# Two-layer hybrid networks on one core: the gate and up products as a 512-column and a 256-column matmul

## What is computed

```python
def swiglu_2(x, w_gate, w_up, w_down):
    return (jax.nn.silu(x @ w_gate) * (x @ w_up)) @ w_down

for i in range(DEPTH):                                   # DEPTH = 2
    g = norm_gains[i]
    f = swiglu_2(rmsnorm_2(h, g[0]), ffn_gate[i, 0], ffn_up[i, 0], ffn_down[i, 0])
    h = h + MACARON * rmsnorm_2(f, g[1])
    ...
    f = swiglu_2(rmsnorm_2(h, g[4]), ffn_gate[i, 1], ffn_up[i, 1], ffn_down[i, 1])
    h = h + MACARON * rmsnorm_2(f, g[5])
```

## Time and profile before

| | |
|---|---|
| median of 3 runs | 1739.27 us (1738.97 to 1739.59) |
| the profiled execution's own time | 1738.88 us |
| span of its trace | 1737.2 us |
| granted TensorE clock, mean | 0.993 |
| PE busy | 1688.1 us (97%), 11882 matmuls |
| DVE busy | 1177.2 us (68%) |
| ACT busy | 897.5 us (52%) |
| DMA | 353.80 MB, mean 204 GB/s |

### The profile page before, as it was taken

How to read it: one execution, slowest core, us unless ns; L and a number is a source line. 1 busy time by engine, 2 the same in 40 slices (tenths; PEclk the granted TensorE clock), 3 DMA queues, 4 the chain that set the end, 5 groups by cost and what they waited for, 6 DMA issues and landing times.

```text
span 1737.2 us, 30015 instructions
## 1 busy us (share of the span) xinstructions
PE 1688.1 (97%) x11882; PEld 1574.2 (91%) x11882; DVE 1177.2 (68%) x1485; ACT 897.5 (52%) x1240; POOL 110.2 (6%) x161
## 2 busy tenths in 40 slices
PE   6999999999999999999999999999999999999997
PEld 4987999998899998999898899999999999899997
DVE  7999789867764458655776755577655575765556
ACT  4567443366544345434577534356434468644446
POOL 3010211100200000000011000000000003000000
PEclk9999999999999999999999999999999999999999
DMA  9894899947555554554441554544555452455551
GB/s 380 319 336 162 287 357 384 377 161 294 193 195 189 175 192 158 194 190 175 170 156 72 175 200 173 190 166 175 176 190 190 169 183 74 141 205 177 192 187 68
DMA packets 61924, 353.80 MB, mean 204 GB/s; under 512 B 6522, under 2 KB 9738, under 8 KB 27792
## 3 DMA queue, kind: packets, MB, share of 16 engines
q1 hardware_dynamic: 40064, 281.24, 45.1%
q0 software_dynamic: 18384, 66.66, 10.4%
q10 hardware_dynamic: 3392, 4.72, 0.9%
HBM read 349.45 MB, written 3.15 MB: 203 GB/s over the span
## 4 chain that ended last, share of the span: by engine, by line
PE 83%; DVE 9%; DMA 3%; issue 2%; ACT 2%; POOL 1%; DVEq 0%; SPq 0%; POOLq 0%; ACTq 0%
PE bank L501 25%; PE bank L502 25%; PE bank L503 25%; DVE w_lo L1595 2%; PE bank L533 2%; PE bank L535 2%; PE bank L534 2%; PE bank L688 1%; DMA work<-bias_rows 1%; DVE shared L1617 1%; DMA raw<-in_stream 1%; DVE work L1979 1%; POOL work L488 1%; PE bank L701 1%; DVE x L2193 0%
## 5 line engine op out<-in xcount | busy, mean ns | idle before, releaser
L501 PE MATMUL bank<-a_hi,w_hi 128*128 128x256 f32 x2648 | 755.0, 285 | 12.3 <-DVE a_lo L1766 4.4
L503 PE MATMUL bank<-a_hi,w_lo 128*128 128x256 f32 x2648 | 752.0, 284 | 0.0
L502 PE MATMUL bank<-a_lo,w_hi 128*128 128x256 f32 x2648 | 751.9, 284 | 0.0
L501 PEld LDWEIGHTS bank<-a_hi,w_hi 128*128 128x128 f32 x2648 | 510.9, 193 | 18.1 <-issue 10.3
L502 PEld LDWEIGHTS bank<-a_lo,w_hi 128*128 128x128 f32 x2648 | 511.0, 193 | 2.5 <-issue 0.2
L503 PEld LDWEIGHTS bank<-a_hi,w_lo 128*128 128x128 f32 x2648 | 510.7, 193 | 0.0
L1865 DVE TENSOR_TENSOR w_lo<-raw,w_hi 128x2048 fp32r<-128x2048 f32 x144 | 330.0, 2292 | 241.8 <-ACT w_hi L1184 241.8
L1184 ACT CAST w_hi<-raw 128x2048 fp32r<-128x2048 f32 x144 | 274.1, 1903 | 270.6 <-PE bank L503 270.6
L1595 DVE TENSOR_TENSOR w_lo<-raw,w_hi 128x2048 fp32r<-128x2048 f32 x122 | 279.2, 2292 | 80.9 <-ACT w_hi L1043 80.6
L1043 ACT CAST w_hi<-raw 128x2048 fp32r<-128x2048 f32 x121 | 229.7, 1907 | 56.2 <-PE bank L503 47.5
L501 PE MATMUL bank<-w_hi,hid_hi 128*128 128x512 f32 x548 | 214.7, 392 | 0.0
(11 more groups left out here) (259 smaller groups left out, 1872.4 us busy)
## 6 DMA issues: line engine op xcount, KB each, us to landing
raw<-in_stream SPq DMA_DIRECT2D x266, 1024.0 KB, 4.8
shared<-in_mods POOLq DMA_DIRECT2D x104, 512.0 KB, 6.9
grow<-in_rows POOLq DMA_DIRECT2D x12, 512.0 KB, 4.0
work<-in_mods POOLq DMA_DIRECT2D x8, 512.0 KB, 8.9
bias_rows<-work ACTq DMA_DIRECT2D x1, 2048.0 KB, 20.6
x<-in_x_t SPq DMA_DIRECT2D x1, 1024.0 KB, 5.9
x<-in_x_d ACTq DMA_DIRECT2D x1, 1024.0 KB, 6.2
work<-bias_rows ACTq DMA_DIRECT2D x1, 1024.0 KB, 18.4
```

What stands on the lines that cost most here:

```text
L501: pe.matmul(out, w_h, v_h, start=start, stop=False, skip_group_check=True)
L502: pe.matmul(out, w_h, v_l, start=False, stop=False, skip_group_check=True)
L503: return pe.matmul(out, w_l, v_h, start=False, stop=stop, skip_group_check=True)
```

## The change

Three things, all in the FFNs i = 2 to 5.

1. `a_hi` and `a_lo` become the two halves of one tile `a_both`, so that a chunk's high and low activations lie side by side, 512 columns. A new `wide_slab` takes the place of `feature_slab` for gate and up slabs: per chunk and m one matmul of 512 columns (high weights by high and low activations) and one of 256 columns (low weights by high activations) onto its first half. The two m now have a bank each, so a gate slab fills banks 0 and 1, an up slab 2 and 3, without a second pair. `two_sums` views a pair as (m, token, half).
2. VectorE first adds the two halves (`tensor_reduce`, 1024 sums to 512 numbers, into `gate_s` or `hid`) and counts `gate_summed` or `up_summed`; it then scales those in place. TensorE waits for these counts before the next gate or up slab.
3. VectorE's order: at an FFN's start the gate's addition stands ahead of two `w_lo` slabs and `pre_root` ahead of these; at its end `hidden_lo` stands ahead of the last `w_lo`.

```diff
-        bank = [ctx.enter_context(nc.psum_tensor(f"bank{i}", [P, 512], F32)) for i in range(8)]
+        bank_pair = [ctx.enter_context(nc.psum_tensor(f"banks{i}", [P, 1024], F32)) for i in range(4)]
+        bank = [bank_pair[i // 2][:, 512 * (i % 2):512 * (i % 2) + 512] for i in range(8)]
+
+        def two_sums(b):
+            return bank_pair[b][:, :].rearrange("p (m k s) -> p m s k", m=2, k=2)
...
-        a_hi = sb("a_hi", [P, LCH, S], F32R)
-        a_lo = sb("a_lo", [P, LCH, S], F32R)
+        a_both = sb("a_both", [P, LCH, 2, S], F32R)
+        a_hi, a_lo = a_both[:, :, 0, :], a_both[:, :, 1, :]
...
+            def wide_slab(slot, pair_of_banks, chunk_ready=None):
+
+                for c in range(CH):
+                    if chunk_ready is not None:
+
+                        pe.wait_ge(nl_ready, chunk_ready + c + 1)
+                    for m in range(2):
+                        w_h, w_l = weights(slot, c * 256 + m * P, P)
+                        out = bank[2 * pair_of_banks + m]
+                        pe.matmul(out[:, :], w_h, a_both[:, c].rearrange("p k s -> p (k s)"), start=(c == 0), stop=False, skip_group_check=True)
+                        mm = pe.matmul(out[:, 0:S], w_l, a_hi[:, c, :], start=False, stop=(c == CH - 1), skip_group_check=True)
+                return mm
...
+                        if i > 1:
+
+                            pe.wait_ge((gate_summed, up_summed)[k], (1 if j is None else j) + (f0 - 2 * FJ))
+                            wide_slab(slot + k, k).then_inc(slab_done, 1)
+                            continue
...
-                    feature_slab(b, bank[0], before(APPLY_CHUNKS, ap)).then_inc(slab_done, 1)
+                    wide_slab(b, 0, before(APPLY_CHUNKS, ap)).then_inc(slab_done, 1)
                     pe.wait_ge(lo_ready, b + 2)
-                    feature_slab(b + 1, bank[2]).then_inc(slab_done, 1)
+                    wide_slab(b + 1, 1).then_inc(slab_done, 1)
...
+                    dve.tensor_reduce(pair(gate_s[:, par, :]), two_sums(0), mybir.AxisListType.X, ALU.add).then_inc(gate_summed, 1)
...
+                    dve.wait_ge(gate_summed, j + (f0 - 2 * FJ + 1))
+                    dve.tensor_tensor(pair(gate_s[:, par, :]), pair(gate_s[:, par, :]), over_pre(), ALU.mult).then_inc(gate_scaled, 1)
...
-                        dve.tensor_tensor(pair(hid[:, par, :]), pair(bank[2 + par][:, :]), over_pre(), ALU.mult).then_inc(up_scaled, 1)
+                        dve.tensor_reduce(pair(hid[:, par, :]), two_sums(1), mybir.AxisListType.X, ALU.add).then_inc(up_summed, 1)
+                        dve.wait_ge(up_summed, j + (f0 - 2 * FJ + 1))
+                        dve.tensor_tensor(pair(hid[:, par, :]), pair(hid[:, par, :]), over_pre(), ALU.mult).then_inc(up_scaled, 1)
...
+                gate_sum(0, 0, b + 1, True)
                 split_to(b + 4)
                 if i == 0:
                     mod_half()
-                gate(0, 0, b + 1, True)
+                gate_scale(0, 0, True)
...
                 hidden(j, j % 2, b + 3 * j + 1)
-                split_to(b + 3 * j + 4)
+                if i < 2:
+                    split_to(b + 3 * j + 4)
                 hidden_lo(j, j % 2)
+                if i >= 2:
+                    split_to(b + 3 * j + 4)
...
                 turned_low(apply2(l, LA_PRE1), gain2(l, 0))
-                split_to(base2(l) + 3)
+                split_to(base2(l) + 2)
                 pre_root(4 * l)
-                split_to(base2(l) + 4)
                 ffn(2 + 2 * l, base2(l))
```

More of the change, by code:

```diff
@@ L352, in build @@
         gate_scaled, up_scaled = sem("gate_scaled"), sem("up_scaled")
+        gate_summed, up_summed = sem("gate_summed"), sem("up_summed")
         table_ready = sem("rope_over_rms_ready")
@@ L1831, in ffn, with gate_sum @@
                 v = 4 * ((i - 2) // 2) + (0 if i % 2 == 0 else 2)
-                def gate(j, par, done, first=False):
+                def gate_sum(j, par, done, first=False):
                     if i < 2:
@@ L1839, in gate, with gate_scale @@
                         dve.wait_ge(hid_done, j + (f0 - 1))
+                    dve.tensor_reduce(pair(gate_s[:, par, :]), two_sums(0), mybir.AxisListType.X, ALU.add).then_inc(gate_summed, 1)
+                def gate_scale(j, par, first=False):
+                    if i < 2:
+                        return
                     if first:
                         dve.wait_ge(row_ready, rows_made(v))
-                    dve.tensor_tensor(pair(gate_s[:, par, :]), pair(bank[par][:, :]), over_pre(), ALU.mult).then_inc(gate_scaled, 1)
+                    dve.wait_ge(gate_summed, j + (f0 - 2 * FJ + 1))
+                    dve.tensor_tensor(pair(gate_s[:, par, :]), pair(gate_s[:, par, :]), over_pre(), ALU.mult).then_inc(gate_scaled, 1)
+                def gate(j, par, done, first=False):
+                    gate_sum(j, par, done, first)
+                    gate_scale(j, par, first)
                 def hidden(j, par, up, first=False):
@@ L2358, in _ @@
                 turned_low(apply2(l, LA_PRE2), gain2(l, 4))
-                split_to(bf + 3)
+                split_to(bf + 2)
                 pre_root(4 * l + 2)
-                split_to(bf + 4)
                 ffn(3 + 2 * l, bf)
```

## The result

| | kernel before | changed kernel |
|---|---|---|
| time, median of 4 runs each | 1739.43 us (1738.97 to 1740.80) | 1729.30 us (1728.39 to 1731.07) |
| ratio | | 0.9937, 95% interval 0.9916 to 0.9959 |
| profiled execution | 1738.88 us, span 1737.2 | 1728.39 us, span 1726.7 |

The change makes the kernel faster: by 10.1 us (0.6%) between the medians, by 10.5 us in the profiled executions. The forecast was 22.5: right sign, inside the range, less than half the size.

A forecast was written before the change was run, and what follows sets the result against it. TensorE's matmul pace was taken to bound the second network's FFNs: 1738.88 - 23 (matmuls) + 0.5 (start of FFN i = 2) = 1716.4 us profiled, median 1716.8, range 1707 to 1730.

The forecast's parts named there:

- What bounds the kernel: In the second network's FFNs, the time one matmul takes until the next can start on TensorE sets the time.
- The matmuls: In gate and up slabs, two matmuls replace three of 119.9 ns each; 1408 pairs save 23 us, the middle of two readings.
- by neighbours of unlike width: Pair cost in wide slabs read from single steps between unlike widths: 340 ns, 19.7 saved, 27.7 us in all.
- by the steady runs: Pair cost in wide slabs read from runs of one width: 346.6 ns, 13.1 saved, 18.4 us in all.
- the end at 351.6 ns: Outer pair cost in wide slabs if every 512 costs what a run's first six do: 8.1 ns or 11.4 us saved.
- VectorE's additions: Additions of 1.28 us each on DVE hide beside TensorE in the FFN loop, with 3.8 and 4.2 us to spare.
- The end of an FFN: Behind the last up slab, `hidden_lo` ends at 4.5 us, wanted at 5.5, with the moved `w_lo` needed; cost 0.
- the rival of the seams: If an addition takes 2.56 us, FFN ends lose 0.4 us each and starts up to 2: 1719 to 1727; 7%.
- The start of an FFN: The gate's addition ahead of two `w_lo`, with rope angles in FFN i = 2, costs 0.5 us, once.
- The time by columns: Rival for wide slabs: time goes by columns, only a ns or two per matmul falls away; 1736 to 1739.3; 5%.
- VectorE the bound: Rival: strided additions make DVE the loop's bound; about 3.7 us each eats the gain, 4 gives about 1774 us; 3%.

The follow-up runs named there:

- e1: Changed kernel with three matmuls of 256 columns per product again in place of the wide and narrow pair; 1743.27 us (1 run).
- e2: Changed kernel with VectorE copying the first half of each bank pair instead of adding both halves; 1727.19 us (1 run).
- e4: Changed kernel with each slab's sixteen 512-column matmuls first, then its sixteen of 256 columns; 1724.76 us (4 runs), ratio to before 0.9916.
- e8: Changed kernel with the last `w_lo` put back ahead of `hidden_lo` at the end of the four FFNs; 1738.28 us (1 run).
- e7: Changed kernel with every VectorE addition done twice, once into a spare tile, 2.45 us for 1.22; 1753.46 us (1 run).
- e5: Changed kernel, widths still alternating, but each 256-column matmul goes to the other group's bank than the 512 ahead of it; 1727.98 us (1 run).
- e6: Changed kernel with two 512-column matmuls, then their two of 256 columns, all four into one bank; 1727.60 us (1 run).
- f2: Changed kernel with two 512-column matmuls of a chunk, then its two of 256 columns; 1724.97 us (6 runs), ratio to before 0.9912.

## Why the prediction was right or wrong, point by point

- **What bounds the kernel: right.** TensorE's starts set the time. `e1` and `e2` show it from both sides: DVE's additions come and go without moving a turn but the one behind the second rope angle.
- **The matmuls: this step failed.** "I take the middle, 23 us" put the pair at 343 ns. It costs 352.8 in the loop, so 1408 pairs save 9.7 us. The mechanism held (a matmul less in three, with some 13 ns that do not depend on width), the size did not. The reading "by neighbours of unlike width" (340 ns) added two steps that the rows give at 0.01 us and that each occur once, at a change of slab; the first pair behind a down slab does cost 340, the later ones don't. The reading "by the steady runs" (346.6 ns) describes a kernel that groups its widths: `e4` has 346.9. The alternating order costs 6 ns more than that in the loop, and 13 more than the other reading. What came out is nearest to the end at 351.6 ns, which the forecast had kept for the range: in the earlier trace rows the first six wide matmuls behind narrow ones take 231.7. That row was the only one in which a wide matmul had a changed neighbourhood for some time, and it said the cost goes up. It should have drawn the value up, not stood as an outer end.
- **VectorE's additions: right.** 1.22 us for 1.28, and hidden in the loop. Doubled, they stay hidden in 32 of 36 turns; the four others are first or second turns of an FFN. The forecast took 1280 ns as the nearest row; the trace of before also has 1226 for two inputs of 1024 (L2256), nearer to the 1223 measured.
- **The end of an FFN: right in the result, wrong in the account.** The moved `w_lo` is needed (`e8`, 5.8 us). But the slack is about 0.25 us and not the 1.0 that 4.5 and 5.5 leave, as the forecast let the addition start 0.28 behind the up slab, with DVE free. That the chain still fitted was luck. DVE is in the next slab's `w_lo` then, which stands at the end of the chain gate addition, scaling, silu, cast. `e7` paid for it: up to 3.1 us of waiting for 1.2 more per addition. In the rival of the seams the price at R = 2.56 ("0.4 us each") was wrong by the same step: at 2.45 us the four ends of `e7` wait 2.8 each on the average.
- **The start of an FFN: right.** 0.5 us charged, 0.38 seen in the turn behind the second rope angle. `e7` shows how little more it bears.
- **The time by columns: excluded.** A pair costs 6.9 ns less than three narrow ones. By N / 2.4 + 2.5 ns, as the page "TensorE: Matmul & The Clock Gate" of the Trainium skill has it (section "Back-to-back issue gap"), the pair would be 325.0 ns and the saving 2.5 a pair, both estimates; the trace differs from them, 352.8 and 6.9.
- **VectorE the bound: excluded** for this addition (1.22 us, far below the 3.7 needed). At 2.45 us `e7` was already slower than before, 1753.46 against 1738.51 us (1 run each), with 17.7 us of waits at the ends and starts of the FFNs and 32 of 36 turns covered. So the point from which the rival decides was put too high.

## What to carry to other kernels

A matmul's price depends on its neighbours: where an edit puts unlike widths side by side, take the pace from rows with such neighbours for a while, and let the dearest of them set the middle, not the edge. Where matmuls of two widths add into the same sums, try them in groups first; here the groups brought 4.7 to 5.9 ns a pair on top of the 6.9 of the removed matmul. Before an edit lengthens a step, follow the chain on the engines that feed it at the place with the least cover (here one down slab), for the step may stand behind a wait that idle time elsewhere doesn't show.

## What the runs showed that had not been expected

- **Order of widths.** In the loop, 512 and 256 columns in turn: 352.8 ns a pair. Two and two: 348.1. Sixteen and sixteen: 346.9. The bank written to makes no difference (`e5`, `e6`).
- **Two paces of one order.** In the changed kernel, every pair of slabs that follows a down slab without a stop runs at 352.8 ns. Of those behind a stop of PE or behind a short piece of other work, the ones at 658.7, 670.3, 704.2 and 966.5 us run at 347 behind their first pair and the ones at 978.0, 1203.4 and 1512.8 at 353, all at full clock. At the slower pace the pairs' times repeat by threes, 350, 350 and 360 ns, where at 704.2 every pair takes 346 to 348. So the order alone does not fix the pace; what chooses is open, and no run here tried it.
- **Short half-clock stretches** (1.2 GHz) in an otherwise full clock, from none (`f2`) to 17 us in all (`e7`) from the start of FFN i = 2 on, at places that change from one execution to the next. Between runs of one kernel they come to several us, as much as this change gives, so its turns (0.01 us apart between executions) tell more than its times.
